# Two-layer hybrid decoder step on one core: down products of an expert pair moved behind the next pair's gate and up products, an earlier first product, a norm in three pieces

## The reference, cut to what matters

```python
gidx = top1(x @ rg_w + rg_b)              # 1 of 4 groups
eidx = top2(x @ re_w + re_b, in group)    # 2 of its 8 experts
hid  = silu(x @ w_gate[e]) * (x @ w_up[e])      # 1024 -> 256
out  = sum over the two e of gate[e] * (hid @ w_down[e])   # 256 -> 1024
h    = layer_norm(ALPHA * h + out)
```

## Time and profile before

| What | Value |
|---|---|
| Median of 3 runs (lowest to highest) | 1221.47 us (1219.94 to 1226.11) |
| The profiled execution: its time | 1217.85 us |
| its span in the profile | 1216.1 us |
| PE busy | 1056.4 us, 87% |
| DVE busy | 623.6 us, 51% |
| ACT busy | 338.8 us, 28% |
| POOL busy | 201.7 us, 17% |
| Moved by transfers | 284.19 MB, mean 234 GB/s |
| Chain that ended last | PE 64%, transfers 16%, DVE 12% |

### The profile page before, as it was taken

The page is one execution under the profiler, slowest core; times in us unless marked ns, Lnnn a source line. Parts: engine busy times, 40 slices in busy tenths (PEclk is TensorE's granted clock), DMA queues, the critical chain, the costliest instruction groups (busy, mean ns, idle before and its releaser), DMA issues.

```text
span 1216.1 us, 16340 instructions
## 1 busy us (share of the span) xinstructions
PE 1056.4 (87%) x5237; PEld 610.7 (50%) x5237; DVE 623.6 (51%) x1102; ACT 338.8 (28%) x518; POOL 201.7 (17%) x335
## 2 busy tenths in 40 slices
PE   6999999992899778789999899899928997899996
PEld 5999996541333222234577677665413332233342
DVE  2232323347364434442749999773483644455526
ACT  2222121002243322331321231450023433334420
POOL 5333330000112111112400000000001121122230
PEclk8999999996899888899999899999968998899999
DMA  9362102029999999986714111300299999999855
GB/s 303 96 174 70 47 24 106 35 91 376 384 400 417 396 388 395 406 336 231 255 34 138 30 70 43 125 14 34 91 376 383 397 403 389 405 403 362 357 171 191
DMA packets 74652, 284.19 MB, mean 234 GB/s; under 512 B 15787, under 2 KB 34431, under 8 KB 48831
## 3 DMA queue, kind: packets, MB, share of 16 engines
q1 hardware_dynamic: 58312, 242.63, 51.8%
q10 hardware_dynamic: 5383, 20.85, 4.9%
q0 software_dynamic: 10912, 20.10, 4.4%
HBM read 273.53 MB, written 27.26 MB: 247 GB/s over the span
## 4 chain that ended last, share of the span: by engine, by line
PE 64%; DMA 16%; DVE 12%; issue 3%; ACT 2%; SPq 2%; ACTq 1%; DVEq 0%; POOL 0%; POOLq 0%
PE ps L1242 15%; PE ps L1061 14%; PE ps L1093 11%; DMA ring<-in_moe_w_down_dram 8%; PE ps L1257 8%; PE ps L1077 5%; DMA ring<-in_moe_w_up_dram 5%; PE ps L1170 3%; DVE arena L1824 2%; DVE ring L1824 2%; PE ps L1228 2%; DMA arena<-x_rows_dram,now 1%; PE ps L1352 1%; PE ps L1119 1%; DMA ring<-in_x_sample_dram 1%
## 5 line engine op out<-in xcount | busy, mean ns | idle before, releaser
L1242 PE MATMUL ps<-arena 128*64 128x512 f32 x1152 | 271.8, 627 | 40.6 <-DVE arena L1691 38.4
L1242 PEld LDWEIGHTS ps<-arena 128*64 128x64 f32 x1152 | 86.9, 145 | 220.9 <-issue 158.4
L1690 DVE COPY arena<-ring 128x1024 f32 x144 | 99.2, 689 | 111.6 <-SPq L575 69.7
L1257 PE MATMUL ps<-arena 128*64 128x512 f32 x576 | 131.5, 598 | 21.3 <-DVE arena L1707 21.3
L1093 PE MATMUL ps<-ring 128*128 128x512 f32 (+1 forms) x320 | 141.1, 593 | 0.7 <-ACT ring L901 0.7
L1077 PE MATMUL ps<-arena,ring 128*128 128x296 f32 x512 | 131.4, 418 | 7.1 <-DVE arena L1802 4.7
L1077 PEld LDWEIGHTS ps<-arena,ring 128*128 128x128 f32 x512 | 98.1, 193 | 38.6 <-DVE arena L1802 5.2
L684 ACT COPY arena<-ring 128x1024 f32 x72 | 75.1, 1044 | 140.2 <-SPq L575 61.7
L1691 DVE COPY arena<-ring 128x1024 f32 x144 | 98.8, 686 | 0.0
L1061 PE MATMUL ps<-hT_hi,w_hi 128*128 128x296 f32 x384 | 86.5, 307 | 6.7 <-PE ps L1061 6.7
L1093 PEld LDWEIGHTS ps<-ring 128*128 128x128 f32 (+1 forms) x320 | 56.7, 182 | 69.4 <-issue 69.0
(11 more groups left out here) (277 smaller groups left out, 1196.7 us busy)
## 6 DMA issues: line engine op xcount, KB each, us to landing
ring<-in_moe_w_gate_dram SPq DMA_DIRECT2D x64, 1024.0 KB, 8.0
ring<-in_moe_w_up_dram SPq DMA_DIRECT2D x64, 1024.0 KB, 10.3
ring<-in_moe_w_down_dram SPq DMA_DIRECT2D x64, 1024.0 KB, 10.7
ring<-in_sc_w_in_dram SPq DMA_DIRECT2D x12, 1024.0 KB, 13.3
ring<-y_rows_dram ACTq DMA_DIRECT2D x6, 1024.0 KB, 7.8
ring<-in_cf_w_pw_dram SPq DMA_DIRECT2D x4, 1536.0 KB, 16.2
ring<-in_sc_w_out_dram SPq DMA_DIRECT2D x2, 2048.0 KB, 7.8
x_rows_dram<-ring ACTq DMA_DIRECT2D x8, 512.0 KB, 2.6
```

Source lines behind the costliest of these rows:

```text
L1242: ins = nc.tensor.matmul(ps[own, B_GU, :], xT_e[:, k, own], w_gu[:, x, c, i * 2 * F:(i + 1) * 2 * F], start=(k == 0), stop=(k == C - 1))
L1257: ins = nc.tensor.matmul(ps[own, B_Y + half, :], hidT[:, k, own], w_dn[:, x, k, half * DH:(half + 1) * DH], start=(k == 0), stop=(k == FK ...
L1690: nc.vector.tensor_copy(as_gu(w_gu[:, 0, c, :]), gu_chunk(ranks[0], c))
```

## The change

- In the expert loops PE's order becomes `gate_up(s+1)`, `turn_x(s+2)`, `down(s)`, `turn_hid(s+1)`; DVE's `multiply(s+1)`, `copy_gu(s+2)`, `copy_y(s)`, `copy_hidT(s+1)`; ACT's silu, `copy_xT(s+1)`, `copy_dn(s)`. First and last steps are written out apart. POOL's part is not touched.
- SP asks for gate and up first for all slots.
- The first product begins when tiles 0 to 2 are copied, on the first half of the tokens; its weights are split between the copies of tiles; the 7 filler products are gone; a product goes through the halves of the tokens outside, not inside. Tiles 2 and 3 swap banks. SP waits for the tokens ahead of the second and third piece of the first slot.
- The norm goes in pieces of 128, 168 and 296 tokens; ACT does its part of the first piece before the state rows; 24 filler products in place of 44.

```diff
@@ turn_bank
-            return B_TURN - 2 * (m % 4) if m < NT else B_TURN
+            return (6, 4, 0, 2)[m % 4] if m < NT else B_TURN
...
+        NORM_PIECES = [(0, slice(0, P)), (0, slice(P, HALF)), (1, slice(HALF, T))]
...
+        def duo_behind_last(eng):
+
+            return eng.value_load(tab[0:1, T_LAST + 1:T_LAST + 2], min_val=PAIRS // P - 2, max_val=NDUO - 2)
@@ SP
                 if n == 0:
                     sp.dma_start(*pieces[0]).then_inc(first_loaded, 16)
+                    for t in range(NT):
+                        sp.wait_ge(h_loaded[t], 16 if 0 < t < NT - 1 else 32)
...
-                down_first = upto is not None and r % SLOTS < 2
-                for part in (down, gate_up) if down_first else (gate_up, down):
+                for part in (gate_up, down):
...
-                    if n == 1:
-
-                        for t in range(NT):
-                            sp.wait_ge(h_loaded[t], 16 if 0 < t < NT - 1 else 32)
@@ ACT
                 def body(s, first=False, final=False):
 
-                    if not first:
-                        copy_dn(s, record(mybir.EngineType.Activation, s), first)
                     act.wait_ge(gu_used[l], NCH * s + NCH)
...
                     if not final:
                         copy_xT(s + 1)
+                    if not first:
+                        copy_dn(s, record(mybir.EngineType.Activation, s), first)
...
                 copy_hT(t)
+                if NT - 3 <= t < NT - 1:
+                    split_hi(PRODUCTS[0][0], (t - (NT - 3),))
...
+                mix_piece(0)
                 state_rows(1, SB)
...
+                mix_piece(1)
+                mix_piece(2)
@@ PE
-                    for kc in range(KC):
-                        k = c * KC + kc
-                        for w, x in ((w_hi, hT_hi), (w_hi, hT_lo), (w_lo, hT_hi)):
-                            for a in range(2):
+                    for a in range(2):
+                        if i == 0:
+                            tiles = -(-HALF // P) if a == 0 else NT
+                            pe.wait_ge(hT_act, tiles)
+                            pe.wait_ge(hT_dve, tiles)
+                        for kc in range(KC):
+                            k = c * KC + kc
+                            for w, x in ((w_hi, hT_hi), (w_hi, hT_lo), (w_lo, hT_hi)):
...
-                    pe.wait_ge(b_mixed, C if t * P + n <= HALF else 2 * C)
+                    pe.wait_ge(b_mixed, C * sum(own.start < t * P + n for _, own in NORM_PIECES))
...
                 turn_hid(0)
+                gate_up(1, False)
+                turn_x(2)
                 down(0, True)
-                with pe.Fori(1, last) as s:
-                    gate_up(s, False)
-                    turn_x(s + 1)
-                    turn_hid(s)
+                turn_hid(1)
+                with pe.Fori(1, last - 1) as s:
+                    gate_up(s + 1, False)
+                    turn_x(s + 2)
                     down(s, False)
+                    turn_hid(s + 1)
                 gate_up(last, False)
+                down(duo_behind_last(pe), False)
                 turn_hid(last)
                 down(last, False)
...
-            pe.wait_ge(hT_act, NT)
-            pe.wait_ge(hT_dve, NT)
...
-                if p.index == 0:
-                    pe.wait_ge(hT_act, 2)
-                    pe.wait_ge(hT_dve, 2)
-                    keep_busy(4, 7)
...
-            keep_busy(B_TURN, 44)
+            keep_busy(B_TURN, 24)
@@ DVE
                 copy_hidT(0)
+                multiply(1, False)
+                copy_gu(2, record(mybir.EngineType.DVE, 2), False)
                 copy_y(0, True)
-                with dve.Fori(1, last) as s:
-                    multiply(s, False)
-                    copy_hidT(s)
-                    copy_gu(s + 1, record(mybir.EngineType.DVE, s + 1), False)
+                copy_hidT(1)
+                with dve.Fori(1, last - 1) as s:
+                    multiply(s + 1, False)
+                    copy_gu(s + 2, record(mybir.EngineType.DVE, s + 2), False)
                     copy_y(s, False)
+                    copy_hidT(s + 1)
                 multiply(last, False)
                 dve.sem_inc(products_over, 1)
+                copy_y(duo_behind_last(dve), False)
                 copy_hidT(last)
                 copy_y(last, False)
...
-            for a, own in enumerate(halves_of):
+            for i, (a, own) in enumerate(NORM_PIECES):
```

More of the change, by code:

```diff
@@ L638, in copy_hT, with split_hi @@
                 last.then_inc(hT_act, 1)
-            def split_hi(p):
+            def split_hi(p, halves=(0, 1)):
                 if p.index == 0:
@@ L645, in split_hi @@
                     act.wait_ge(weights_ready, p.n + 1)
-                for c in range(2):
+                for c in halves:
                     i = 2 * p.index + c
@@ L714, in _ @@
                 copy_hT(t)
+                if NT - 3 <= t < NT - 1:
+                    split_hi(PRODUCTS[0][0], (t - (NT - 3),))
             for p in PRODUCTS[0]:
-                split_hi(p)
+                if p.index:
+                    split_hi(p)
                 if p.index == 1:
@@ L894, in _, with mix_piece @@
                     nc.scalar.activation(rstd_sb[:, own], rstd_sb[:, own], ACT.Sqrt, bias=eps[:, 0:1]).then_inc(csd_ready, 1)
+                def mix_piece(i):
+                    own = NORM_PIECES[i][1]
+                    for j in range(C):
+                        act.wait_ge(normed, C * i + j + 1)
+                        nc.scalar.activation(mixT[:, j, own], mixT[:, j, own], ACT.Silu, bias=cln_b(j),
+                                             scale=cln_g(j)).then_inc(b_mixed, 1)
+                mix_piece(0)
                 state_rows(1, SB)
@@ L1857, in _ @@
                 for j in range(C):
-                    dve.wait_ge(centred, 4 + C * a + j + 1)
+                    dve.wait_ge(centred, 4 + C * i + j + 1)
                     nc.vector.tensor_tensor(mixT[:, j, own], mixT[:, j, own], rstd_sb[:, own], ALU.mult).then_inc(normed, 1)
```

## The result

The changed kernel takes 1329.68 us (median of 4 runs, 1322.01 to 1336.47) where the kernel before, beside it on the same chip, takes 1221.87: a ratio of 1.0875, 95% interval [1.0809, 1.0942]. It is slower, and the time lies in the range of the prediction, 35 us under the predicted one. The profiled execution took 1330.61, its span is 1327.7 against 1216.1, so 111.6 us are to be found.

| Stretch | Before | After | Difference |
|---|---|---|---|
| start to the first gather of layer 0 | 298.1 | 291.5 | -6.7 |
| expert loop of layer 0, first gather to last store | 266.3 | 306.6 | +40.2 |
| last store to the first gather of layer 1 | 341.5 | 344.7 | +3.3 |
| expert loop of layer 1 | 271.9 | 346.6 | +74.7 |
| rest | 38.3 | 38.4 | +0.1 |

A forecast was written before the change was run, and what follows sets the result against it. Expert loops bound by weights at the transfers' rate, by PE where weights are there. Profiled 1217.85, loops +147.3 (+57.2 and +90.1), start -4, other edits 0: 1361; median 3.6 above: 1365 us, range 1295 to 1415.

The forecast's parts named there:

- The cause: Expert loops: gather of s+3 queues behind the store of s, which waits for moved down products; +147.3 us over both layers.
- L: Time from a token-row gather's issue to its landing in the expert loops: 7.8 us, 5.8 for a layer's last gather.
- The low clock: PE at 1.2 GHz behind each wait for rows: turn 1.97 us, down products 5.3, instead of 1.09 and 3.65.
- GpSimd's gap: From the end of the store's issue to the gather's issue: 0.78 us plus a gap of 0.2, together 0.98.
- The start: First product starts earlier, without fillers and at the low clock: -4 us, bounds 0 and -6.1.
- The norm: Norm in three pieces: first projection up to 5.7 us earlier, possible clock loss 2.6; taken as 0, bounds -5.7 and +2.6.
- SyncE's later down weights: Down-weight loads and those behind them start up to 6.87 us later, covered by ring slots: 0, upper bound 14 us.
- The milder loop: Rival 1's milder part: gathers late, but landing in 5.8 us at full clock, steps of 14.8: 1240 to 1280 us; chance 0.08.
- The second wanted landings of 2.6: Rival 2: gathers meet empty queues and land in 2.6 us, steps of 12.85 against 12.56: 1221 us, no change; chance 0.04.
- The faster rival: Rival 3: rows are there in time (landing below 2.0 us, or store not holding gather), PE paces: 1210 us; chance 0.06.
- 11.97 a step: PE's own work in one expert-loop step, in us, once the 0.59 wait for the hidden copy is removed from 12.56.
- The signs: Trace marks if right: 5 us waits before row turns, clock below 0.9, steps of 17 to 21, first product ending near 26.

The follow-up runs named there:

- the gather ahead: The changed kernel with GpSimd issuing the gather of rows s+3 before the store of pair s: 1243.72 us, ratio 1.0176.
- the light kernels: Expert loads after a layer's first five cut to an eighth: kernel before 1175.67 us, changed kernel 1243.44, changed kernel with gather before store 1163.74.
- the gather ahead and the later requests: Changed kernel with gather before store, and SyncE asking for an expert's down weights behind the next expert's gate and up: 1450.56 us, ratio 1.1896.

## Why the prediction was right, and where its terms were off

- **The cause** was named as it is: the gather of s+3 behind the store of s, a closed loop through PE, Vector, GpSimd and a landing. Shown by the timeline, and by 86 us given back when the gather goes ahead.
- **L**, forecast 7.8: the measured median is 7.6, and 17.9 less the other terms gives 7.7. The number is right, its reason only in part: the gather was to meet a full queue at 386 GB/s, and the loops move 328 and 291, at 230 in the later half of layer 1 with landings of 7.4 all the same. That the number held there is partly luck.
- **The low clock**, forecast 1.97 + 5.3 = 7.27 in every step: measured 6.35 and 6.66. At 1137.76 the granted clock is 0.50 (1.2 GHz) in the turn but 0.84 in the down products, where the forecast kept all 5.26 us low. It follows most holes but not all, and covers more or less of what comes: turns of 1.97 stand before down products of 4.1 to 5.8, turns of 1.16 before 5.35 or 3.65. 0.6 to 0.9 too much.
- **GpSimd's gap**, forecast 0.98 from the end of the store's issue to the gather's issue: measured 0.62 (1147.25 to 1147.87). The gap of 0.2 is not there (1147.25 to 1147.26), and from the index copy to the issue it is 0.61, not 0.78. 0.36 too much.
- Together the step was put at 19.3 and is 17.9 and 18.2. Over 13 and 15 steps that is 18 and 17 us; the loops were forecast at +57.2 and +90.1 and came to +40.2 and +74.7, 17.0 and 15.4 less. This one sum, above all its clock term, is where the middle of the prediction missed.
- **The start**, -4 with bounds 0 and -6.1: -6.7 at the first gather, beyond the bound; the eleven other traces with this start have that gather 3.0 to 7.2 us earlier than the kernel before. The first product begins at 15.93, as forecast (16.1), but at full clock (granted 1.00 from 15.93 to 23), not the low one: its 48 matmuls come 0.14 apart and end at 23.0, where 26.5 was the forecast. The forecast took the low clock because no filler runs ahead; the transposes now run right up to the product. In the kernel before, the fillers and the first part of the product themselves ran at 0.50 (18.91 to 24.5), behind a gap of 1.81. The second waits 1.52 for its weights and begins at 25.74, before at 31.13. As a part of the whole time, with the old loops, it is some 4 (1220.34 to 1216.19); what becomes of the other 2 to 3 us is not shown.
- **The norm**, 0: right by the traces. The first projection does come sooner behind the first subtraction (831.91 to 838.2, 6.3 us for 10.0), and the rest of the stretch takes it back. The 3.3 us between the loops lie ahead of it: the wait for the first result rows after layer 0 is 3.10 for 1.30, and the combination's first products take 8.80 for 7.10, slow behind that wait. From the first product of layer 1's mixer to the first gather the traces agree, 302.1 (640.60 to 942.74) and 302.1 (603.84 to 905.91). The 6.9 us between the medians of the start with and without the norm lie elsewhere and stay open.
- **SyncE's later down weights**, 0 with an upper bound of 14: in the change PE shows no wait for weights, so 0 held there. With the gather ahead, so that the late rows no longer cover it, the loops lose 29 us, of which 13 in the stream, near that bound but not shown to be SyncE's pause, and 15 in the drain, which the prediction did not price: the moved down products themselves stand behind the last weights.
- **The rivals.** The milder loop (L of 5.8, full clock) did not come: the landings stayed long (median 7.6) although the queue was not full. The second wanted landings of 2.6, and no gather of any run took less than 3.0. The faster rival fails at its condition, as said; the light kernels show that even with that condition met the gain is a few us a layer. Its 11.97 a step was too low as well: 12.12 is what PE takes there. PE also paced early steps of the loop before, not the last alone (four gathers from 332.41 to 382.62 come 12.55 apart), but there, by the forecast, the weights end last in any case; no run here takes that apart.
- **The signs** it named came, but for two: PE waits 4.1 us on average before a turn (5 forecast), the granted clock is 0.87 in both loops, single steps take 14.8 to 21.3 us (17 to 21 forecast); the store's issue precedes the gather's by 1.66, not 2 to 3, and the first product ends at 23.0, not 26.

## What to carry to other kernels

When work is moved later on one engine, follow what it releases through every in-order queue, also those that the change leaves alone: a request that stands behind a wait for the moved work becomes part of a loop, and that loop's length is the sum round it, landing included. A short wait that the profile shows in every step is worth removing only in the steps that this engine paces, and two pieces of work drawn together at the end of a loop pay for it in the drain. If requests are reordered, count what stays under way between a request and the landing that the same queue waits for.

## What the runs showed of the hardware that was not expected

- A row gather of 512 KB lands in 7.6 us (median) in the change, in 8.4 beside the fuller stream with the gather ahead, and in 4.4 with an eighth of the weights; never under 3.0 in any run. The mean rate does not set it: with the gather ahead and the later requests, at 257 GB/s (340 to 600), the median of layer 0 is 3.7, and in the change, at 230 (1120 to 1285), it is 7.4.
- Moving the request for one of an expert's three loads one place back, with a wait for a landing in the same queue, took the kernel from 1243.72 to 1450.56 us, and the rate to 240 to 280 GB/s.
- PE's clock falls behind holes that look short beside a step: in the change the turn took 1.97 after a hole of 3.79, at a granted clock of 0.50, and 1.16 after one of 1.27, at 1.00. Turn and down products then run in part at half speed, while the gate and up products behind them are at full clock again (7.09, granted 1.00, with fillers or without).
